# A square root on ScalarE and a reciprocal on VectorE in place of Ln and Exp, in all RMS norms of a three-block kernel

## The chip, the cores and the metric

The kernel runs on one core of a Trainium2 chip. The metric is the device time of one execution in microseconds (us), taken as the median of several runs; lower is better. The engines are named as in the profile: PE is TensorE, ACT is ScalarE, DVE is VectorE, POOL is GpSimd and SP is SyncE, which issues the DMAs here.

## The reference

Three different residual blocks are applied one after the other to x, 512 tokens by 1024 channels, in float32: one with a gated linear recurrence and a convolution, one with three mixers, one with two delta-rule recurrences. Before each mixer or feed-forward part, and at the end of each block, the rows of x are normalised; inside the third block the 64-wide heads of some tensors are normalised too (to unit length, or to unit mean square). All of these have one core:

```python
def _rmsnorm(x, g):
    xf = x.astype(jnp.float32)
    y = xf * lax.rsqrt(jnp.mean(xf * xf, axis=-1, keepdims=True) + EPS)
    return (y * g.astype(jnp.float32)).astype(x.dtype)

def _modulate(x, g, shift, scale):
    return _rmsnorm(x, g) * (1 + scale) + shift
```

## The kernel before

Channels lie on the 128 partitions and the 512 tokens on the free axis, so that x is `K.xT` with 8 slices of 128x512, and its normalised, modulated copy is `K.hT`. The program is a row of phases. Each phase is a `Block` with one instruction list for each engine, and the order within each list is that of the code. The next block's work starts when every engine has ended its list of this one, so a phase costs what its slowest engine costs. Semaphores order the engines within a phase.

Two helpers are concerned. `norm_phase` normalises whole rows. It is called nine times: at the start of the first block (there with two jobs, x of width 512 and the context of width 256), before its second mixer and at its end; at the start of the second block, before its MLP and at its end; and the same three places of the third block. At the start of the third block POOL builds masks for the recurrences in the same phase (`on_pool`). A phase runs so: ACT loads an activation table (L394) and squares the 8 slices (L400); PE sums over the partitions with a matrix of ones (L420); ACT takes Ln of the mean (L404) and Exp of -0.5 times that (L406), which is 1/sqrt; DVE multiplies the 8 slices by the gain and by that factor (L435); ACT adds the shift (L411), except in the final norms.

`head_norm_phase` does the same for heads, with one 128x512 slice as a job: `nk3` has 4 jobs, `lnx` 4 (with a subtraction of the mean first, L2154), `l2` 8 and `on` 4. For job n ACT squares (L2144), PE sums (L2127), ACT does Ln (L2135) and Exp in place (L2137) into one of two buffers `rs`, DVE multiplies (L2157). ACT squares job n+1 before it takes the root of job n. After `nk3` and after `l2` comes `delta_phase`, whose ACT list begins with Exp activations (L2365, L2360); after the first `norm_phase` comes `hgrn_phase`, whose ACT list begins with an Exp (L617). None of these three has a table load of its own in the code.

`preload_act_table_set` asks for a table load by name. Where the code asks for none, the compiler places the loads.

Of the kernel before, what the change touches and what calls it, by code (L numbers as in the profile page):

```python
# [9 lines left out]
ACT = mybir.ActivationFunctionType  # L10
AX = mybir.AxisListType
P = 128
DM = 1024
# [4 lines left out]
LOG_EXP_SET = "natural_log_exp_and_others"  # L18
# [41 lines left out]
def clear_old(sp, old):  # L60

    for s in old:
        sp.sem_clear(s)
# [305 lines left out]
def norm_phase(K, jobs, on_pool=None):  # L369


    nc = K.nc
    with ExitStack() as st:
        sq = K.sb(st, "norm_sq", [P, 2, T])
        gain = K.sb(st, "norm_gain", [P, len(jobs), KD])
        root = K.sb(st, "norm_root", [P, len(jobs), T])
        rstd = K.sb(st, "norm_rstd", [P, len(jobs), T])
        ps = K.psum_banks(st, "norm")
        sems, old = K.phase()
        squared, summed, rooted, inverted, gained, scaled, added, chain = sems[:8]  # L380
        wide = K.sb(st, "norm_masks", [P, 9, P]) if on_pool else None
        with nc.Block() as block:
            @block.sync
            def _(sp):
                clear_old(sp, old)

            if on_pool:
                @block.gpsimd
                def _(pool):
                    on_pool(K, pool, wide, *sems[8:11])  # L390

            @block.scalar
            def _(act):
                act.preload_act_table_set(LOG_EXP_SET)  # L394
                n = 0
                for j, (x, dst, w, *_) in enumerate(jobs):
                    for k in range(KD):
                        if n >= 2:
                            act.wait_ge(summed, n - 1)
                        act.activation(sq[:, n % 2, 0:w], x[:, k, 0:w], ACT.Square).then_inc(squared, 1)  # L400
                        n += 1
                for j, (x, dst, w, *_) in enumerate(jobs):
                    act.wait_ge(summed, KD * (j + 1))
                    act.activation(root[:, j, 0:w], ps[j][:, 0:w], ACT.Ln, scale=1.0 / DM, bias=K.epsc[:, 0:1]).then_inc(rooted, 1)  # L404
                    act.wait_ge(rooted, j + 1)
                    act.activation(rstd[:, j, 0:w], root[:, j, 0:w], ACT.Exp, scale=-0.5).then_inc(inverted, 1)  # L406
                for j, (x, dst, w, g, shift, scale, v) in enumerate(jobs):
                    if shift is not None:
                        for k in range(KD):
                            act.wait_ge(scaled, KD * j + k + 1)  # L410
                            act.activation(dst[:, k, 0:w], dst[:, k, 0:w], ACT.Identity,  # L411
                                           bias=K.mod[:, shift + k, v:v + 1]).then_inc(added, 1)

            @block.tensor
            def _(pe):
                n = 0
                for j, (x, dst, w, *_) in enumerate(jobs):
                    for k in range(KD):
                        pe.wait_ge(squared, n + 1)
                        pe.matmul(ps[j][:, 0:w], K.ones[:, :], sq[:, n % 2, 0:w], start=(k == 0), stop=(k == KD - 1)).then_inc(summed, 1)  # L420
                        n += 1

            @block.vector
            def _(dve):
                for j, (x, dst, w, g, shift, scale, v) in enumerate(jobs):
                    if shift is None:
                        dve.tensor_copy(gain[:, j, :], K.vec[:, g:g + KD]).then_inc(gained, 1)
                    else:
                        dve.scalar_tensor_tensor(gain[:, j, :], K.mod[:, scale:scale + KD, v], 1.0, K.vec[:, g:g + KD],
                                                 ALU.add, ALU.mult).then_inc(gained, 1)  # L430
                dve.wait_ge(gained, len(jobs))
                for j, (x, dst, w, g, shift, scale, v) in enumerate(jobs):
                    dve.wait_ge(inverted, j + 1)
                    for k in range(KD):
                        dve.scalar_tensor_tensor(dst[:, k, 0:w], x[:, k, 0:w], gain[:, j, k:k + 1], rstd[:, j, 0:w],  # L435
                                                 ALU.mult, ALU.mult).then_inc(scaled, 1)
# [1664 lines left out]
def head_norm_phase(K, tag, jobs, eps, mean_of, center=False):  # L2101


    nc = K.nc
    with ExitStack() as st:
        sq = K.sb(st, tag + "_sq", [P, 2, T])
        rs = K.sb(st, tag + "_rs", [P, 2, T])
        ps = K.psum_banks(st, tag)
        sems, old = K.phase()
        mean, cen, sqd, summed, root, inv, done = sems[:7]  # L2110
        with nc.Block() as block:
            @block.sync
            def _(sp):
                clear_old(sp, old)

            @block.tensor
            def _(pe):
                if center:
                    for n, (x, _) in enumerate(jobs):
                        if n >= 2:  # L2120
                            pe.wait_ge(cen, n - 1)
                        pe.matmul(ps[n % 2][:, :], K.two[:, :], x, start=True, stop=True).then_inc(mean, 1)
                for n in range(len(jobs)):
                    pe.wait_ge(sqd, n + 1)
                    if n >= 2:
                        pe.wait_ge(root, n - 1)
                    pe.matmul(ps[2 + n % 2][:, :], K.two[:, :], sq[:, n % 2, :], start=True, stop=True).then_inc(summed, 1)  # L2127

            @block.scalar
            def _(act):  # L2130
                def root_of(n):
                    act.wait_ge(summed, n + 1)
                    if n >= 2:
                        act.wait_ge(done, n - 1)
                    act.activation(rs[:, n % 2, :], ps[2 + n % 2][:, :], ACT.Ln, scale=1.0 / mean_of, bias=eps[:, 0:1]).then_inc(root, 1)  # L2135
                    act.wait_ge(root, n + 1)
                    act.activation(rs[:, n % 2, :], rs[:, n % 2, :], ACT.Exp, scale=-0.5).then_inc(inv, 1)  # L2137
                act.preload_act_table_set(LOG_EXP_SET)
                for n, (x, _) in enumerate(jobs):
                    if center:  # L2140
                        act.wait_ge(cen, n + 1)
                    if n >= 2:
                        act.wait_ge(summed, n - 1)
                    act.activation(sq[:, n % 2, :], x, ACT.Square).then_inc(sqd, 1)  # L2144
                    if n >= 1:
                        root_of(n - 1)
                root_of(len(jobs) - 1)

            @block.vector
            def _(dve):  # L2150
                if center:
                    for n, (x, _) in enumerate(jobs):
                        dve.wait_ge(mean, n + 1)
                        dve.scalar_tensor_tensor(x, ps[n % 2][:, :], -1.0 / C, x, ALU.mult, ALU.add).then_inc(cen, 1)  # L2154
                for n, (x, gain) in enumerate(jobs):
                    dve.wait_ge(inv, n + 1)
                    dve.scalar_tensor_tensor(x, x, gain, rs[:, n % 2, :], ALU.mult, ALU.mult).then_inc(done, 1)  # L2157

# [528 lines left out]
```

## Time and profile before

| | |
|---|---|
| median of 3 runs | 4726.74 us (4717.89 to 4729.1) |
| the profiled execution | 4729.1 us, span 4727.4 us |
| PE busy | 4004.8 us, 85% of the span |
| DVE busy | 1669.1 us, 35% |
| ACT busy | 1308.1 us, 28% |
| POOL busy | 603.2 us, 13% |
| granted PE clock, mean | 0.905 of full |

The span is what the profiler's records cover; the time lies 1.7 us above it. The share of an engine is a mean over phases with very different limits.

### The profile page before, as it was taken

Reading aid. Unit: us, or ns where it says so; the run is one execution under the profiler, and the core shown is the slowest. Engines: PE = TensorE matmul, PEld = TensorE weight load, DVE = VectorE, ACT = ScalarE, POOL = GpSimd, SP = SyncE. Lnnn points to the kernel's source line nnn. Section 1 sums busy time; section 2 is a strip of 40 time slices with the busy share of each in tenths; the row PEclk is TensorE's granted clock in tenths of the full one; section 3 lists DMA queues with packets and bytes.
Section 4 is the critical chain, followed back from the end, with each engine's and each line's share of the span. In section 5 each row is a group of like instructions: output and inputs, shape, how many; then the busy total and the mean of one; then the engine's idle time right before and its main releaser. Section 6 shows DMA issues by size and latency. Waiting matters only on the chain. (4 is left out here: it accounts for less than half of the span.)

```text
span 4727.4 us, 61028 instructions
## 1 busy us (share of the span) xinstructions
PE 4004.8 (85%) x23891; PEld 2693.9 (57%) x23891; DVE 1669.1 (35%) x3008; ACT 1308.1 (28%) x2192; POOL 603.2 (13%) x326
## 2 busy tenths in 40 slices
PE   6789999999689997778889977988678667877987
PEld 2356666666464443344465555866438447665765
DVE  1024444444516994123213322111227455032222
ACT  0133333333421122222113333222331231324322
POOL 0000000000020000010000022433410110333432
PEclk7799999999899998889869988988889789988998
DMA  8921111111024220112021112322110100222322
GB/s 319 352 62 41 40 44 40 41 44 44 18 58 120 72 71 18 50 36 58 16 55 45 28 53 76 98 76 71 40 29 3 46 10 21 71 71 80 92 72 67
DMA packets 484430, 312.98 MB, mean 66 GB/s; under 512 B 28236, under 2 KB 441477, under 8 KB 484262
## 3 DMA queue, kind: packets, MB, share of 16 engines
q1 hardware_dynamic: 484262, 310.67, 22.3%
q8 instruction: 113, 1.85, 0.2%
q14 instruction: 55, 0.45, 0.0%
HBM read 308.54 MB, written 2.10 MB: 66 GB/s over the span
## 5 line engine op out<-in xcount | busy, mean ns | idle before, releaser
L541 PE MATMUL hg_bank<-hT,hg_w 128*128 128x512 f32 x1024 | 447.3, 592 | 0.0
L998 PE MATMUL cv_bank<-hT,cv_w 128*128 128x512 f32 x768 | 334.0, 596 | 14.1 <-DMA cv_w<-in_conv_w_in_dram 14.1
L541 PEld LDWEIGHTS hg_bank<-hT,hg_w 128*128 128x128 f32 x1024 | 193.3, 190 | 223.6 <-issue 221.9
L1072 DVE SCALAR_TENSOR_TENSOR conv_u<-cv_pad,vec,conv_u 128x512 f32<-128x512 f32 x480 | 318.7, 743 | 0.0
L998 PEld LDWEIGHTS cv_bank<-hT,cv_w 128*128 128x128 f32 x768 | 146.8, 191 | 199.7 <-issue 184.8
L850 PE MATMUL m_bank<-m_rh,m_wh 128*128 128x512 f32 x512 | 205.0, 400 | 63.9 <-POOL m_wl L834 63.9
L851 PE MATMUL m_bank<-m_rl,m_wh 128*128 128x512 f32 x512 | 203.6, 398 | 0.0
L852 PE MATMUL m_bank<-m_rh,m_wl 128*128 128x512 f32 x512 | 203.4, 397 | 0.0
L834 POOL TENSOR_TENSOR m_wl<-m_w,m_wh 128x1024 fp32r<-128x1024 f32 x64 | 152.5, 2386 | 286.3 <-ACT m_wh L866 286.3
L1675 PE MATMUL at_bank<-hT,at_w 128*128 128x512 f32 x384 | 177.1, 605 | 0.0
L834 POOL TENSOR_TENSOR ho_wl<-ho_w,ho_wh 128x2048 fp32r<-128x2048 f32 x8 | 36.6, 4578 | 1079.3 <-ACT ho_wh L866 1079.3
L850 PE MATMUL ff_bank<-ff_rh,ff_wh 128*128 128x512 f32 x352 | 139.1, 395 | 32.8 <-POOL ff_wl L834 32.8
L755 DVE COPY hg_probe<-hg_bank 128x1 f32<-128x1 f32 x32 | 5.1, 158 | 447.0 <-PE hg_bank L556 447.0
L850 PEld LDWEIGHTS m_bank<-m_rh,m_wh 128*128 128x128 f32 x512 | 99.2, 194 | 87.4 <-issue 66.4
L852 PE MATMUL ff_bank<-ff_rh,ff_wl 128*128 128x512 f32 x352 | 137.9, 392 | 0.0
L851 PE MATMUL ff_bank<-ff_rl,ff_wh 128*128 128x512 f32 x352 | 137.9, 392 | 0.0
L537 PE MATMUL hg_bank<-hg_w,hT 128*128 128x128 f32 x1024 | 119.3, 278 | 16.5 <-DMA hg_w<-in_hgrn_w_in_dram 16.5
L537 PEld LDWEIGHTS hg_bank<-hg_w,hT 128*128 128x128 f32 x1024 | 119.1, 195 | 24.1 <-DMA hg_w<-in_hgrn_w_in_dram 16.9
L834 POOL TENSOR_TENSOR ff_wl<-ff_w,ff_wh 128x1024 fp32r<-128x1024 f32 x44 | 104.0, 2384 | 181.9 <-ACT ff_wh L866 181.9
L420 PE MATMUL norm_bank<-norm_sq,ones 128*128 128x512 f32 (+1 forms) x160 | 90.0, 721 | 40.8 <-ACT norm_sq L400 40.5
L1380 PE MATMUL ml_bank<-hT,ml_w 128*128 128x512 f32 x256 | 118.9, 616 | 3.6 <-ACT ml_o L1442 3.0
L314 PE MATMUL ada_bank<-ada_w,ada_cond 128*32 128x512 f32 x480 | 90.5, 893 | 32.2 <-DMA ada_w<-in_w_ada_dram 26.2
(668 smaller groups left out, 8001.3 us busy)
## 6 DMA issues: line engine op xcount, KB each, us to landing
ada_w<-in_w_ada_dram SPq DMA_DIRECT2D x24, 2048.0 KB, 19.6
hg_w<-in_hgrn_w_in_dram SPq DMA_DIRECT2D x80, 512.0 KB, 3.7
m_w<-in_w_mlp_dram SPq DMA_DIRECT2D x64, 512.0 KB, 4.1
ada_w<-in_ada_w_dram SPq DMA_DIRECT2D x12, 2048.0 KB, 19.8
cv_w<-in_conv_w_in_dram SPq DMA_DIRECT2D x48, 512.0 KB, 3.9
ff_w<-in_w_ffn_in_dram SPq DMA_DIRECT2D x44, 512.0 KB, 4.9
at_w<-in_w_in_dram SPq DMA_DIRECT2D x24, 512.0 KB, 3.9
fo_w<-in_w_ffn_out_dram SPq DMA_DIRECT2D x16, 704.0 KB, 4.7
```

Source lines behind the costliest of these rows:

```text
L314: ins = pe.matmul(ps[s][g:g + 32, :], cond[:, k, :], w[s][:, k, :], start=(k < COLS), stop=(k >= KD - COLS))
L420: pe.matmul(ps[j][:, 0:w], K.ones[:, :], sq[:, n % 2, 0:w], start=(k == 0), stop=(k == KD - 1)).then_inc(summed, 1)
L537: ins = pe.matmul(bank[:, t * P:(t + 1) * P], src[:, k, t * P:(t + 1) * P], W[m][:, k, :], start=(k == 0), stop=(k == KD - 1))
L541: ins = pe.matmul(bank[:, 0:w], W[m][:, k, :], src[:, k, 0:w], start=(k == 0), stop=(k == KD - 1))
L834: ins = pool.tensor_tensor(WL[s % 2][g][:, :, :], W[s % raws][g][:, :, :], WH[s % 2][g][:, :, :].bitcast(F32), ALU.subtract)
L850: pe.matmul(ps[p * 4 + g][:, :], WH[p][g][:, k, :], rh[:, k, :], start=(k == 0), stop=False)
L851: pe.matmul(ps[p * 4 + g][:, :], WH[p][g][:, k, :], rl[:, k, :], start=False, stop=False)
L852: ins = pe.matmul(ps[p * 4 + g][:, :], WL[p][g][:, k, :], rh[:, k, :], start=False, stop=(k == kt - 1))
L998: ins = pe.matmul(ps[n % RING][:, :], W[n % SLOTS][:, k * P:(k + 1) * P], K.hT[:, k, :], start=(k == 0), stop=(k == KD - 1))
L1072: ins = dve.scalar_tensor_tensor(o, x, by, o, ALU.mult, ALU.add)
L1380: ins = pe.matmul(SIDE_BANK[n % 2][:, :], W[n % WS][:, k, :], K.hT[:, k, :], start=(k == 0), stop=(k == KD - 1))
L1675: ins = pe.matmul(SIDE_BANK[:, :], W[n % WS][:, k, :], K.hT[:, k, :], start=(k == 0), stop=(k == KD - 1))
```

## The change

In both helpers the explicit load of the table set with Ln and Exp goes, Ln and Exp become one Sqrt on ACT, and DVE takes the reciprocal of its result ahead of the multiplications, and waits for its own reciprocal.

```diff
@@ norm_phase
-                act.preload_act_table_set(LOG_EXP_SET)
...
                     act.wait_ge(summed, KD * (j + 1))
-                    act.activation(root[:, j, 0:w], ps[j][:, 0:w], ACT.Ln, scale=1.0 / DM, bias=K.epsc[:, 0:1]).then_inc(rooted, 1)
-                    act.wait_ge(rooted, j + 1)
-                    act.activation(rstd[:, j, 0:w], root[:, j, 0:w], ACT.Exp, scale=-0.5).then_inc(inverted, 1)
+                    act.activation(root[:, j, 0:w], ps[j][:, 0:w], ACT.Sqrt, scale=1.0 / DM, bias=K.epsc[:, 0:1]).then_inc(rooted, 1)
...
                 for j, (x, dst, w, g, shift, scale, v) in enumerate(jobs):
+                    dve.wait_ge(rooted, j + 1)
+                    dve.reciprocal(rstd[:, j, 0:w], root[:, j, 0:w]).then_inc(inverted, 1)
                     dve.wait_ge(inverted, j + 1)
@@ head_norm_phase
-                    act.activation(rs[:, n % 2, :], ps[2 + n % 2][:, :], ACT.Ln, scale=1.0 / mean_of, bias=eps[:, 0:1]).then_inc(root, 1)
-                    act.wait_ge(root, n + 1)
-                    act.activation(rs[:, n % 2, :], rs[:, n % 2, :], ACT.Exp, scale=-0.5).then_inc(inv, 1)
-                act.preload_act_table_set(LOG_EXP_SET)
+                    act.activation(rs[:, n % 2, :], ps[2 + n % 2][:, :], ACT.Sqrt, scale=1.0 / mean_of, bias=eps[:, 0:1]).then_inc(root, 1)
...
                 for n, (x, gain) in enumerate(jobs):
+                    dve.wait_ge(root, n + 1)
+                    dve.reciprocal(rs[:, n % 2, :], rs[:, n % 2, :]).then_inc(inv, 1)
                     dve.wait_ge(inv, n + 1)
```

## Rows read from the trace of the kernel before

**Rows 1.** The page: busy time, share of the span, instructions.
```profile
PE 4004.8 (85%) x23891; PEld 2693.9 (57%) x23891; DVE 1669.1 (35%) x3008; ACT 1308.1 (28%) x2192; POOL 603.2 (13%) x326
```
**Rows 2.** Timeline, two `norm_phase` in turn: start, duration, instruction, [idle before <-releaser].
```profile
3333.48 1.28 ACT L394 ACT_TABLE_LOAD   x1 [11.03 <-PEq L813]
...
3344.58 0.69 ACT L404 ACTIVATE norm_root<-norm_bank,epsc 128x512 f32<-128x512 f32 x1 [1.22 <-PE norm_bank L420]
3345.30 0.63 ACT L406 ACTIVATE norm_rstd<-norm_root 128x512 f32<-128x512 f32 x1
3346.05 5.39 DVE L435 SCALAR_TENSOR_TENSOR xT<-xT,norm_gain,norm_rstd 128x512 f32<-128x512 f32 x8 [12.36 <-ACT norm_rstd L406]
...
3351.72 1.28 ACT L394 ACT_TABLE_LOAD   x1 [5.79 <-PEq L382]
...
3366.32 5.70 ACT L411 ACTIVATE hT<-hT,mod 128x512 f32<-128x512 f32 x8 [0.89 <-DVE hT L435]
...
3376.77 0.38 POOL L252 TENSOR_SCALAR neg_up_strict<-up_strict 128x64 f32<-128x64 f32 x1
```
**Rows 3.** Single lines of the kernel: reciprocals, ns min/median/max, first and last start.
```profile
L1517 DVE RECIPROCAL merge_gate<-merge_gate x4: 3353/3353/3353, 2204.6 to 2288.6; 128x512 f32<-128x512 f32 x4
L692 DVE RECIPROCAL hg_lb<-hg_tmp x1: 353/353/353, 260.0 to 260.0; 128x32 f32<-128x32 f32 x1
```
**Rows 4.** Timeline of DVE around a reciprocal in `mlstm_phase`.
```profile
2273.93 3.35 DVE L1517 RECIPROCAL merge_gate<-merge_gate 128x512 f32<-128x512 f32 x1
2277.31 0.69 DVE L1519 TENSOR_TENSOR merge_gate<-ml_bank,merge_gate 128x512 f32<-128x512 f32 x1
```
**Rows 5.** Timeline of `nk3`, 4 jobs: first instructions and last multiplication.
```profile
3532.15 1.28 ACT L2138 ACT_TABLE_LOAD   x1 [12.31 <-PEq L2169]
3533.44 1.15 ACT L2144 ACTIVATE nk_sq<-rw_kk 128x512 f32<-128x512 f32 x2
...
3536.24 0.69 ACT L2135 ACTIVATE nk_rs<-nk_bank,epsc 128x512 f32<-128x512 f32 x1 [1.65 <-PE nk_bank L2127]
3536.96 0.63 ACT L2137 ACTIVATE nk_rs<-nk_rs 128x512 f32<-128x512 f32 x1
...
3542.46 0.69 DVE L2157 SCALAR_TENSOR_TENSOR rw_kk<-rw_kk,nk_rs 128x512 f32<-128x512 f32 x1 [0.63 <-ACT nk_rs L2137]
```
**Rows 6.** Timeline of `l2`, 8 jobs: first Ln, last multiplication.
```profile
3835.25 0.69 ACT L2135 ACTIVATE l_rs<-l_bank,epsc 128x512 f32<-128x512 f32 x1 [1.65 <-PE l_bank L2127]
...
3848.49 0.69 DVE L2157 SCALAR_TENSOR_TENSOR gdn_qkv<-gdn_qkv,l_rs 128x512 f32<-128x512 f32 x1 [0.64 <-ACT l_rs L2137]
```
**Rows 7.** Timeline of `lnx`, 4 jobs.
```profile
3689.03 1.28 ACT L2138 ACT_TABLE_LOAD   x1 [0.49 <-PEq L2232]
3690.92 0.63 ACT L2144 ACTIVATE lnx_sq<-rwkv_y 128x512 f32<-128x512 f32 x1 [0.61 <-DVE rwkv_y L2154]
...
3693.82 0.69 ACT L2135 ACTIVATE lnx_rs<-lnx_bank,eps 128x512 f32<-128x512 f32 x1 [1.41 <-PE lnx_bank L2127]
...
3700.93 0.75 DVE L2157 SCALAR_TENSOR_TENSOR rwkv_y<-rwkv_y,vec,lnx_rs 128x512 f32<-128x512 f32 x1 [1.46 <-ACT lnx_rs L2137]
```
**Rows 8.** Timeline of ACT: loads that the compiler placed, in `token_phase` and a product phase.
```profile
2055.70 0.72 ACT L1193 ACTIVATE tk_sq<-gm_v,tk_sums 128x512 f32<-128x512 f32 x1
...
2056.53 1.28 ACT L1195 ACT_TABLE_LOAD   x1
...
3745.41 1.28 ACT L1936 ACT_TABLE_LOAD   x1 [3.59 <-DVE gdn_qkv L1944]
```
**Rows 9.** Timeline of `delta_phase` after `nk3`: last Exp of slice 0, and DVE.
```profile
3548.68 0.61 ACT L2369 ACTIVATE rw_E<-rw_E 128x512 f32<-128x512 f32 x1
...
3550.28 0.69 DVE L2277 SCALAR_TENSOR_TENSOR rw_EA<-rw_EA,rw_kk 128x512 f32<-128x512 f32 x1
3550.88 0.69 DVE L2278 TENSOR_TENSOR rw_lw<-rw_lw,rw_p 128x512 f32<-128x512 f32 x1
```
**Rows 10.** Windows: busy us of PE, PEld, DVE, ACT, POOL; PEclk; DMA.
```profile
3378.00:3390.00 12.00, 2.77 (x7) 2.23 (x8) 4.92 (x9) 5.86 (x10) 4.66 (x2) 0.50 0.46 126
```

## The prediction

> **What bounds the kernel now.** The page comes first: PE is busy for 85% of the span and DVE for 35% [rows 1]. That average would say that work given to DVE is free. The timeline of a norm phase, read next, says otherwise. In it the reader should follow one path: Ln starts at 3344.58 and ends at 3345.27, Exp ends at 3345.93, DVE's first multiplication starts at 3346.05 after 12.36 us of idling for just that result, its eight end at 3351.44, and at 3351.72 the next phase begins [rows 2]. Nothing else runs meanwhile. So between phases there is no overlap, and what bounds a norm phase is a chain through ACT, PE, ACT and DVE. Whatever the change adds to this chain is added to the time. The same holds in `nk3`: the last Exp's user starts at 3542.46 and the phase ends with it [rows 5].
>
> **The price of a reciprocal.** The kernel already has this instruction in this shape: 128x512 in float32 took 3353 ns four times out of four, and 128x32 took 353 ns [rows 3]. Per element that is (3353 - 353) / 480 = 6.25 ns, so 128x256 comes to about 353 + 224 x 6.25 = 1753 ns (an estimate from these two rows). The user of a reciprocal starts 0.03 us after its end, the semaphore included: 2273.93 + 3.353 = 2277.28, and 2277.31 [rows 4]. Sqrt is taken at the cost of Ln, 0.69 us: same operands, same shape; the trace has no wide Sqrt, but all wide activations on these rows lie between 0.61 and 0.69 us, so the doubt is below 0.1 us per phase.
>
> **`norm_phase`.** Before, from the end of Ln to the first multiplication: 3346.05 - 3345.27 = 0.78 us, of which 0.12 is the step from ACT to DVE [rows 2]. After: 0.12 + 3.353 + 0.03 = 3.50 us. Net +2.72 us for a phase. Of the nine:
> - Seven plain ones: 7 x 2.72 = 19.0 us.
> - The first has a second job, of width 256. DVE works through job 0's eight multiplications before it comes to the second reciprocal, so that lies on the path whole: 2.72 + 1.75 + 0.03 = 4.5 us.
> - The one at the start of the third block costs nothing: ACT's last addition ends at 3372.02, while POOL, building masks in the same phase, ends at 3377.15 [rows 2]. The cover is 5.1 us. If it were gone, the price would be 2.7 us.
>
> Together 23.5 us.
>
> **`head_norm_phase`.** Here every job needs a reciprocal. Before, a job took ACT some 1.7 us (13.24 us from the first Ln to the eighth multiplication [rows 6], less 1.4 for the lead of one job: Ln, Exp and the step to DVE, over 7) and DVE waited for it; after, DVE needs 3.353 + 0.03 + 0.61 = 3.99 us a job where a multiplication takes 0.69 (independent DVE instructions of that length follow each other at 0.60 us [rows 9]; 0.61 is taken) and 4.05 where it takes 0.75 (they follow at (5.39 - 0.75) / 7 = 0.66 [rows 2]; 0.67 is taken). ACT's shortened job, with Exp gone, fits easily under that, and two buffers are enough, since Sqrt of the next job needs 0.69 us while a 3.35 us reciprocal runs. DVE becomes the bound. The end is the end of the first Sqrt + 0.03 + jobs x 3.99 (4.05) + 0.08, the last term because the last multiplication is not overlapped.
> - `nk3`: 3536.93 + 0.03 + 15.97 + 0.08 = 3553.0, before 3543.15 [rows 5]: +9.9 us.
> - `l2`: 3835.94 + 0.03 + 31.94 + 0.08 = 3868.0, before 3849.18 [rows 6]: +18.8 us.
> - `on` has the pattern of `nk3`, with the same 6.22 us from first Ln to last multiplication, and multiplications of 0.75: 0.69 + 0.03 + 16.21 + 0.08 against 6.22 + 0.75 = +10.0 us.
> - `lnx`: like `on`, but its load moves from a hidden place to an open one (below): first Sqrt ends at 3693.82 + 1.28 + 0.69 = 3695.79, so the end is 3712.1, before 3701.68 [rows 7]: +10.4 us.
>
> Together 49.1 us.
>
> **The table loads.** Thirteen explicit loads go, each 1.28 us, and the load of the set with Sqrt is now the compiler's to place. The trace shows where it puts one: directly ahead of the first activation that the present set lacks, behind that activation's wait. In `token_phase` Squares run on the earlier set and the load stands between the last Square and the Sqrt; in a product phase the load starts only after a 3.59 us wait for the data of its Silu [rows 8]. So here it should stand between the wait for PE's sum and Sqrt, open on the path. At the start of `nk3` the removed load is open too, since the Squares follow it at once [rows 5]: -1.28 + 1.28 = 0, and so in most phases. Exceptions: in `lnx` the removed load was half hidden, and the first Square waited for DVE 0.61 us longer anyway [rows 7], so nothing is gained there and 1.28 us is paid (counted above). The second of two norm phases in a row reloads a set that is already there [rows 2]; its load now falls away. That holds for the first norm of the second and third blocks, and for the final norm of the second, behind an MLP whose ACT list needs only Copy and Relu. The third block's is covered by POOL. Gain: 2 x 1.28 = 2.6 us. On the other side three Exp activations lose the set they relied on: L617, a small preparation while the first weights load, nothing; L2365 in `delta_phase`, where the last Exp of slice 0 ends at 3549.29 and DVE turns to its user at 3550.28 without waiting [rows 9]: 3549.29 + 1.28 + 0.03 - 3550.28 = 0.3 us; L2360, where DVE's preparation is as long, 0 to 0.3 us, taken as 0. The bound for these three is 0 to 3.8 us.
>
> What a load costs beside its own length is one point to weigh. After the load in `nk3` the next activation starts 0.01 us after its end (3533.43, 3533.44 [rows 5]). The Trainium skill (ScalarE: Activation LUTs, section "What ACT_TABLE_LOAD costs") gives 1283 ns for the load, which agrees, and adds a drain, 2.66 us for each switch. By that the two saved and the one exposed load would count double, and the sum would be about 1 us smaller. The same page (section "Table sets: the hidden batching unit") speaks against this change: Ln and Exp share one set, and Exp with Sqrt needs two. This trace prices that as the exposed loads just counted.
>
> **The sum.** 23.5 + 49.1 - 2.6 + 0.3 = 70.3 us against the profiled execution's 4729.1 us: 4799.4. This execution is 0.05% above the median of 4726.7, so by the median it would be 4797. I take 4799 us, 1.5% slower.
>
> **The rivals.**
> - *Loads at better places.* If the load runs while ACT waits for PE, each phase whose removed load was open gains 1.28 us: nine such waits, 11.5 us, 4788 us. For it: such an idle wait exists, 1.22 to 1.65 us long [rows 2, 5]. Against: rows 8, where the load came after the wait.
> - *More loads.* If Square is missing in a set that is now active (the sets left behind by Exp, Silu or Sigmoid), the phase gets a load ahead of the Squares as well as one ahead of Sqrt: up to 13 x 1.28 = 16.6 us, 4816 us. Against: Squares in `token_phase` ran on a set left by another function [rows 8].
> - *PE colder.* PE idles some 10 to 20 us longer in the head norms. If work behind them starts at a lower clock, DVE waits for PE in `delta_phase`: an estimate of 0 to 6 us, 4805 us at most. Against: a product phase behind a norm starts at a granted clock of 0.50, the 1.2 GHz level, already now [rows 10], so there is nothing to lose there.
> - *Not slower.* If this reciprocal, on data that Sqrt just wrote, were as fast as DVE's multiplications, 0.69 us, a norm phase would pay 0.06 us for it, DVE's job in a head norm would be 1.33 to 1.39 us against 1.7 now, and with the loads the sum would be about -5 us: 4724, no measurable difference. It decides at 70.3 / 28.5 = 2.47 us less than 3.353, that is below 0.9 us (28.5 reciprocals of full width on the path: 8, a half, and 20). Against: four out of four at 3353 ns, and a narrow one on the same line through them [rows 3].
>
> **How the numbers follow.** The forecast has a chance of 0.74 (4793 to 4806), the better places 0.08, more loads 0.08, the colder PE 0.07, not slower 0.03. Runs of before spread from 4717.9 to 4729.1 us, and a measurement of this kernel tells about 0.3%, 14 us, from no change. The range goes down to the better places less 2 us, 4786, and up close to more loads, 4814. Slower by over 0.3%: 0.97; within: 0.02; faster: 0.01.
>
> **What the profile after would show.** Nine or ten reciprocals of `norm_rstd` and 20 of the `rs` buffers, 3.35 us each in width 512; 3.5 us from the end of Sqrt to the first multiplication; DVE nearly without idle time from the first reciprocal to the last multiplication of a head norm, and 28.5 x 3.35 = some 96 us more on DVE; ACT less by about 18 us; loads at L404 or L2135 behind the wait, no load in the norm phases at the start and the end of the second block and at the start of the third; the norm at the third block's start no longer than before. PE's busy time should not move. The prediction falls if a reciprocal takes clearly less than 3.35 us, if a phase's end turns out to be set by something other than DVE, or if loads appear in the loops of the phases between.

## The result

The changed kernel takes 4781.4 us (median of 4 runs, 4777.7 to 4785.9) against 4726.2 us before: a ratio of 1.012, 95% interval 1.0109 to 1.0133. It is 55 us slower where 73 were forecast by the median (4799 us). The direction is right, and the time lies just under the low end of the range, 4786. The profiled execution is 4788.3 us, 59.2 above the profiled one of before; that pair is what the following accounts for.

The page of the kernel after, busy time, share of the span and instructions, as in [rows 1]:
```profile
PE 4003.1 (84%) x23891; PEld 2695.7 (56%) x23891; DVE 1770.8 (37%) x3038; ACT 1289.8 (27%) x2162; POOL 603.5 (13%) x326
```
DVE has 30 instructions more and 101.7 us more work, ACT 18.3 us less. Single lines of the kernel after, ns min/median/max and first and last start:
```profile
L431 DVE RECIPROCAL norm_rstd<-norm_root x10: 1746/3352/3353, 249.7 to 4767.2; 128x512 f32<-128x512 f32 x9, 128x256 f32<-128x256 f32 x1
L2153 DVE RECIPROCAL l_rs<-l_rs x8: 3344/3346/3353, 3865.9 to 3893.8; 128x512 f32<-128x512 f32 x8
L403 ACT ACT_TABLE_LOAD  x6: 1283/1283/1283, 247.6 to 4765.1; - x6
L2134 ACT ACT_TABLE_LOAD  x4: 1283/1283/1283, 3541.5 to 4036.5; - x4
```
The reciprocals cost what [rows 3] say, and the loads are as many as the forecast had: six in nine norm phases, one in each of the four head norms. What is new is when they run. Timeline of the norm phase ahead of the second mixer, kernel before (it follows busy PE work):
```profile
1394.08 1.28 ACT L394 ACT_TABLE_LOAD   x1 [21.05 <-PEq L813]
1395.37 1.15 ACT L400 ACTIVATE norm_sq<-xT 128x512 f32<-128x512 f32 x2
...
1405.18 0.69 ACT L404 ACTIVATE norm_root<-norm_bank,epsc 128x512 f32<-128x512 f32 x1 [1.22 <-PE norm_bank L420]
```
The same phase after:
```profile
1399.13 1.15 ACT L399 ACTIVATE norm_sq<-xT 128x512 f32<-128x512 f32 x2 [21.07 <-PEq L812]
...
1405.53 0.63 ACT L399 ACTIVATE norm_sq<-xT 128x512 f32<-128x512 f32 x1 [0.23 <-PE norm_bank L417]
1406.17 1.28 ACT L403 ACT_TABLE_LOAD   x1
1407.47 0.69 ACT L403 ACTIVATE norm_root<-norm_bank,epsc 128x512 f32<-128x512 f32 x1
1408.27 3.35 DVE L431 RECIPROCAL norm_rstd<-norm_root 128x512 f32<-128x512 f32 x1 [8.94 <-ACT norm_root L403]
1411.65 5.39 DVE L434 SCALAR_TENSOR_TENSOR hT<-xT,norm_gain,norm_rstd 128x512 f32<-128x512 f32 x8
```
Two things are to be seen. The load starts at 1406.17, straight behind the last Square, with no idle time before it, and it covers the 1.22 us in which ACT waited for PE before. Secondly, from the phase's start to the root it took 11.10 us before and takes 8.34 now: 2.76 less, more than one load of 1.28. The rest is PE's clock. Windows over these two stretches (columns as in [rows 10]), before and then after:
```profile
1394.10:1405.20 11.10, 9.09 (x16) 3.12 (x16) 0.17 (x1) 6.21 (x10) 0.00 (x0) 0.85 0.00 1
```
```profile
1399.10:1407.50 8.40, 7.52 (x16) 2.46 (x16) 0.17 (x1) 6.24 (x10) 0.00 (x0) 1.00 0.00 1
```
One microsecond out of the middle of the first of them:
```profile
1398.00:1399.00 1.00, 1.00 (x3) 0.50 (x2) 0.00 (x0) 0.05 (x1) 0.00 (x0) 0.50 0.00 0
```
PE's sums in both kernels, with its idle time ahead of them:
```profile
1396.05 9.09 PE L420 MATMUL norm_bank<-norm_sq,ones 128*128 128x512 f32 x16 [3.28 <-ACT norm_sq L400]
```
```profile
1399.82 7.52 PE L417 MATMUL norm_bank<-norm_sq,ones 128*128 128x512 f32 x16 [2.01 <-ACT norm_sq L399]
```
Before, the sixteen records of the sums take 9.09 us at a mean granted clock of 0.85 for the stretch, part of them at 0.50, the 1.2 GHz level; after, 7.52 us at 1.00, the 2.4 GHz level throughout. PE stands idle 2.01 us instead of 3.28 between the product before and its first sum. Not every phase gains this. Six norm phases follow busy PE work and have a start like this one, 11.1 us to the root in nearly all of them before. In the first profile of the changed kernel four of the six take 8.3 us to the root, in a second one three; the others take 9.8 to 10.0. From the root to the first multiplication the forecast holds: 1411.65 - 1408.16 = 3.49 us (3.50 forecast).

`nk3` after, the counterpart of [rows 5], and the start of the `delta_phase` behind it:
```profile
3540.38 1.15 ACT L2140 ACTIVATE nk_sq<-rw_kk 128x512 f32<-128x512 f32 x2 [12.45 <-PEq L2167]
...
3541.54 1.28 ACT L2134 ACT_TABLE_LOAD   x1
...
3542.84 0.69 ACT L2134 ACTIVATE nk_rs<-nk_bank,epsc 128x512 f32<-128x512 f32 x1
...
3543.56 3.35 DVE L2153 RECIPROCAL nk_rs<-nk_rs 128x512 f32<-128x512 f32 x1 [3.48 <-ACT nk_rs L2134]
...
3546.95 0.69 DVE L2155 SCALAR_TENSOR_TENSOR rw_kk<-rw_kk,nk_rs 128x512 f32<-128x512 f32 x1
3547.56 3.34 DVE L2153 RECIPROCAL nk_rs<-nk_rs 128x512 f32<-128x512 f32 x1
...
3558.91 0.69 DVE L2155 SCALAR_TENSOR_TENSOR rw_kk<-rw_kk,nk_rs 128x512 f32<-128x512 f32 x1
3559.89 1.28 ACT L2363 ACT_TABLE_LOAD   x1 [7.47 <-PEq L2110]
...
3563.45 0.63 ACT L2363 ACTIVATE rw_EA<-rw_EA 128x512 f32<-128x512 f32 x1 [2.28 <-DVE rw_E L2264]
```
DVE runs without a gap from the first reciprocal on, 3.99 us a job, as forecast. The first root comes 2.46 us after the start, against 4.09 in [rows 5]. The load for Exp, forecast behind its wait at 0.3 us, runs at once when the phase begins and ACT then idles 2.28 us more: it costs nothing.

The whole, from the two timelines. Each of the 13 norm and head-norm phases is cut at its start (its first instruction), its first root, its first multiplication and its end (the end of its last instruction). The last row also holds what lies ahead of the first norm phase, where nothing was changed; that stretch alone is 1.5 us longer here.

| | difference after - before | forecast |
|---|---|---|
| start to first root | -20.9 us | -2.6 for two loads, +1.3 for `lnx` |
| first root to first multiplication | +35.0 us | together with the next row 71.3, |
| first multiplication to end | +37.4 us | with nothing for the phase under POOL |
| everything ahead of, between and behind the phases | +7.7 us | +0.3 |
| sum | +59.2 us | +70.3 |

### The profile page after: what moved, and what is told of

It reads as the page before. It is cut to its first block and busy times, and to the rows that moved or that the text cites. A ratio compares the mean times of both kernels' runs of the same rounds, so it can differ in the third digit from the quotient of the medians.

```text
span 4786.6 us, 61028 instructions
## 1 busy us (share of the span) xinstructions
PE 4003.1 (84%) x23891; PEld 2695.7 (56%) x23891; DVE 1770.8 (37%) x3038; ACT 1289.8 (27%) x2162; POOL 603.5 (13%) x326
## 5 line engine op out<-in xcount | busy, mean ns | idle before, releaser
L540 PE MATMUL hg_bank<-ctxT,hg_w 128*128 128x256 f32 x512 | 115.7, 379 | 0.0
## 6 DMA issues: line engine op xcount, KB each, us to landing
ada_w<-in_w_ada_dram SPq DMA_DIRECT2D x24, 2048.0 KB, 19.6
```

The lines of the kernel that those rows point to most:

```text
L540: ins = pe.matmul(bank[:, 0:w], W[m][:, k, :], src[:, k, 0:w], start=(k == 0), stop=(k == KD - 1))
```

## Experiments

Each is compared with runs of the kernel before on its own chip (4728.95 us in the first four, 4728.41 in the next three). Theory A says that the shortfall comes from where the load stands: hidden in ACT's wait, and with PE reached sooner and so still at its higher clock. Its rivals are B (placement is worth nothing) and C (only the wait, not the clock).

**The load moved, Ln and Exp kept.** Only the explicit load of the kernel before moves.
```diff
-                act.preload_act_table_set(LOG_EXP_SET)      # norm_phase: ahead of the Squares
+                act.preload_act_table_set(LOG_EXP_SET)      # behind them, ahead of wait_ge(summed, ...)
...
+                    if n == 1:                              # head_norm_phase: ahead of the first root
+                        act.preload_act_table_set(LOG_EXP_SET)
```


> The kernel before, with Ln and Exp kept, and only the explicit table load moved: in norm_phase from ahead of the Squares to behind them, in head_norm_phase to just ahead of the first Ln. No reciprocal. Theory A (the shortfall against the forecast comes from where the load stands: it now runs while ACT waits for PE, and PE starts 1.28 us sooner after the phase before and so keeps its clock): about 20 us faster than before, 4702 to 4710 us, and from phase start to first Ln 8.3 us in the norm phases that follow busy PE work, against 11.1. Theory B (the placement is worth nothing, the shortfall comes from other phases or from variation between executions): 4720 to 4730 us. Theory C (only the idle wait is used, the clock stays as it was): 10 to 13 us faster, 4714 to 4717.

4716.9 us, ratio 0.9975 (0.9965 to 0.9985): faster by 12, beating both kernels. Timeline of the same norm phase, and windows over it:
```profile
1395.80 1.15 ACT L399 ACTIVATE norm_sq<-xT 128x512 f32<-128x512 f32 x2 [21.07 <-PEq L813]
...
1402.85 1.28 ACT L401 ACT_TABLE_LOAD   x1
1404.14 0.69 ACT L404 ACTIVATE norm_root<-norm_bank,epsc 128x512 f32<-128x512 f32 x1
```
```profile
1395.80:1404.20 8.40, 7.52 (x16) 2.46 (x16) 0.17 (x1) 6.27 (x10) 0.00 (x0) 1.00 0.00 1
```
8.34 us from start to root, with the clock at 1.00: A's mechanism with no Sqrt and no reciprocal in sight. The 13 phases gained 23 us up to their first root. But the time fell by only 12, so A's number (4702 to 4710) missed; C's number fits while its claim about the clock does not. Of the other 11 us, 3.6 are lost inside the phases, between the first multiplication and the end: the phase under POOL, where POOL ends last, is only 0.5 us shorter for a root 2.5 us sooner, and `nk3` and `on` end only 0.7 us sooner for a root 1.6 us sooner. The rest is lost outside them, and is taken up below.

**The load put back at the start of the changed kernel.**
```diff
+                act.preload_act_table_set(SQRT_SET)         # "sqrt_and_others", first in ACT's list, both helpers
```


> The changed kernel with one thing put back: an explicit load (of the set with Sqrt) at the start of both helpers, where before had its own. Theory A: the 22 us that the phases gained between their start and the first root go again, 4799 to 4806 us, close to the forecast for the change. Theory B: no change, 4778 to 4786 us. Theory C: 4793 us.

4804.1 us, ratio 1.0157 (1.0143 to 1.0171). The same phase:
```profile
1398.66 1.28 ACT L395 ACT_TABLE_LOAD   x1 [21.05 <-PEq L814]
...
1409.76 0.69 ACT L405 ACTIVATE norm_root<-norm_bank,epsc 128x512 f32<-128x512 f32 x1 [1.22 <-PE norm_bank L419]
```
```profile
1398.70:1409.80 11.10, 9.09 (x16) 3.12 (x16) 0.17 (x1) 6.21 (x10) 0.00 (x0) 0.85 0.00 1
```
11.10 us and 0.85 again, and the time is 75 us above before where the changed kernel is 55 above. That lies in A's range and outside those of B and C. The kernel has a load in all 13 phases, three more than the changed one; its price is near the one that the forecast gave to the change.

**The load written out behind the wait**, where the forecast had put it.
```diff
                     act.wait_ge(summed, KD * (j + 1))
+                    if j == 0:
+                        act.preload_act_table_set(SQRT_SET)  # and likewise for job 0 in head_norm_phase
```


> The changed kernel with the load of the set with Sqrt written out, behind the wait for PE's sum, where the forecast put it; in the three norm phases that needed no load there is one now. It parts the two halves of Theory A: PE starts early as in the changed kernel, but the load is not hidden. If hiding the load is worth 1.2 us in each of ten phases with a load, and the three new ones cost 1.3 us in two places (the third lies under POOL): 4791 to 4797 us. If all of the gain were the clock: 4780 to 4785 us.

4795.0 us, ratio 1.0144 (1.0129 to 1.016), in the range named for "hiding counts". Timeline of the same phase:
```profile
1396.24 1.15 ACT L400 ACTIVATE norm_sq<-xT 128x512 f32<-128x512 f32 x2 [21.06 <-PEq L815]
...
1404.47 1.28 ACT L405 ACT_TABLE_LOAD   x1 [1.21 <-PE norm_bank L420]
1405.77 0.69 ACT L406 ACTIVATE norm_root<-norm_bank,epsc 128x512 f32<-128x512 f32 x1
```
Here the load does wait 1.21 us, and start to root is 9.53 us: the clock's 1.57 are gained, the wait's 1.20 are not. The kernel has three loads that the changed kernel does not have. Two of them are open, at the start and at the end of the second block, and its starts there are 1.0 and 1.3 us longer than in the first profile of the changed kernel.

**PE kept busy during the old load.** Kernel before, with filler matmuls ahead of `norm_phase`'s own.
```diff
+                for k in range(4):
+                    pe.matmul(ps[7][:, 0:256], K.ones[:, :], jobs[0][0][:, k, 0:256], start=True, stop=True)
```


> The kernel before, load at its old place, and four matmuls of 128x256 on data at hand ahead of norm_phase's own, into a bank that nobody reads, so that PE is not idle during the load (head_norm_phase is left as it was). It parts the clock from the wait. Theory A: PE's sums run at a granted clock near 1.0 in the phases behind busy PE work, some 1.5 us less in four to six phases, 5 to 9 us faster than before: 4717 to 4722 us. Theory C: 4726 us or a little more. If the filler itself delays the first sum: up to 1 us more a phase, 4735.

4725.7 us, ratio 0.9992 (0.9983 to 1.0001): not told from no change. By its time A missed (4717 to 4722) and C's number fits. In the phase, though, the effect is there:
```profile
1394.67 1.28 ACT L394 ACT_TABLE_LOAD   x1 [21.05 <-PEq L815]
...
1404.21 0.69 ACT L404 ACTIVATE norm_root<-norm_bank,epsc 128x512 f32<-128x512 f32 x1 [1.22 <-PE norm_bank L422]
```
```profile
1394.70:1404.30 9.60, 9.46 (x24) 3.88 (x24) 0.17 (x1) 6.28 (x10) 0.00 (x0) 1.00 0.00 1
```
The load is in its old place, the wait of 1.22 is still there, and yet start to root is 9.54 us. That is the clock alone. All six phases that follow busy PE work take 9.53 us. All phases together gained 11.8 us by this profile, and the interval of its time allows at most 8 of them.

**The reciprocals alone.**
```diff
-                    dve.reciprocal(rstd[:, j, 0:w], root[:, j, 0:w]).then_inc(inverted, 1)   # and rs; DVE reads root itself
-  ... ACT.Sqrt, scale=1.0 / DM, ...
+  ... ACT.Sqrt, scale=0.0, ...
```


> The changed kernel without its reciprocals: DVE multiplies by the output of Sqrt itself, and Sqrt is fed scale 0.0, so that the factor is a constant and values stay bounded. What is left out is the reciprocal and with it the normalisation. It prices the reciprocals alone. If each costs what its timeline shows (8 of 3.38 us and one of 1.78 us in the norm phases, 20 jobs that fall from 3.99 to about 1.2 us in the head norms): 85 us less than the changed kernel, 4694 to 4700 us. If part of the reciprocal's time is given back elsewhere, for instance because PE rests longer and is granted more clock later: less than 75 us, above 4706.

4700.5 us, ratio 0.9936 (0.9922 to 0.995): 81 us under the changed kernel by the medians, 87 by the two ratios (0.0184 x 4726), for 85 expected; the time lies at the upper end of the range named (4700). First and last multiplication of `nk3`:
```profile
3522.88 0.69 DVE L2151 SCALAR_TENSOR_TENSOR rw_kk<-rw_kk,nk_rs 128x512 f32<-128x512 f32 x1 [3.81 <-ACT nk_rs L2132]
...
3527.01 0.69 DVE L2151 SCALAR_TENSOR_TENSOR rw_kk<-rw_kk,nk_rs 128x512 f32<-128x512 f32 x1 [0.63 <-ACT nk_rs L2132]
```
4.13 us for three jobs, where the changed kernel needs 11.96. So a root on ACT with nothing behind it is faster than Ln and Exp; the reciprocal on DVE is what makes the change slow. (This kernel's output is not normalised: it gives a price and is no alternative.)

**Half the change.** Each helper changed alone.

> norm_phase as changed, head_norm_phase as before. By the forecast's terms (every reciprocal on the path, 7 x 2.72 + 4.5, less 2.6 for loads): 21 us slower than before. By Theory A (in the trace of the changed kernel the nine phases lose about 23 us to reciprocals that are not covered by POOL, and gain 16 us between their start and the first root): 6 to 10 us slower, and within what the profile's other stretches vary.

> head_norm_phase as changed, norm_phase as before. By the forecast's terms: 49 us slower than before. By Theory A (48 us for the reciprocals by the trace, less 5.6 us between start and first root): 42 us slower, plus what the delta phases lose when PE comes to them colder, 0 to 6 us.

`norm_phase` alone: 4740.8 us, ratio 1.0025 (1.0016 to 1.0034), 12 us. `head_norm_phase` alone: 4768.4 us, ratio 1.0091 (1.0075 to 1.0106), 40 us. The forecast had 21 and 49, Theory A 6 to 10 and 42; the first lies 2 us above A's range. Together the halves make 52 of the 55 us, so they add. Three quarters of the loss are the 20 jobs of the head norms.

**Repeated profiles**, to find out what the stretches between the phases are.

> The kernel before once more, for a second profile: by how much the stretches between the norm phases vary from one execution to the next. If the 9.6 us that these stretches took longer in the profile of the changed kernel are variation, this one differs from the first profile by some us too; if they are an effect of the change, it agrees with the first within 2 us.

> The kernel of late_load once more, for a second profile. Its phases gained 23 us between their start and the first root, its time only 12. If the rest (9 us in the stretches between the phases) is given back there because of the change, this profile shows the same 9 us, against a new profile of before; if it is variation, the stretches sum to within 4 us of those of before.

> As the run before this one: a third profile of the same kernel, same expectations.

> The kernel before for a third profile, to which the two are compared: the sum of its stretches between the phases within 4 us of the first two profiles of before.

> The changed kernel for a second profile. Between start and first root the phases take the same as in the first profile within 3 us; if the 8 us more in the stretches between are an effect of the change they are here again, if variation they are not.

Their times: before 4726.8 and 4725.5, the moved load 4714.7 and 4723.1, the changed kernel 4787.4 us. Sums from the timelines, us; the last column holds everything outside the 13 phases:

| kernel, profiles | start to first root | outside the phases |
|---|---|---|
| before, 3 | 124.6, 124.6, 126.0 | 4491.9, 4490.3, 4487.7 |
| load moved, 3 | 101.4, 101.4, 99.9 | 4500.0, 4497.2, 4507.0 |
| changed, 2 | 103.7, 102.9 | 4499.6, 4498.7 |

Both columns hang on the kernel more than on the execution, which moves the second by up to 10 us (one stretch of before took 924.5 us in the first profile and 920.0 and 919.5 in the others). The expectation for the third profile of before, within 4 us of the other two, missed by 0.2. Against the mean of before, 4490.0, part of the gain up to the root is given back each time: 10, 7 and 17 us with the load moved, 10 and 9 in the changed kernel. The stretch ahead of the first norm phase moves by itself between 231.3 and 235.6 us. Without it, before takes 4259.7, 4256.0 and 4254.8, the kernel with the moved load 4265.9, 4265.9 and 4271.4, and the changed kernel 4265.8 and 4265.1. But `norm_phase` alone (4258.3), `head_norm_phase` alone (4253.1) and the changed kernel with its load behind the wait (4258.1) give nothing back, while the changed kernel without reciprocals (4265.6) and the one with its load at the start (4264.4) do, each in one profile. One place is the `delta_phase` behind `l2`: 136.9 to 137.1 us in all three profiles of before, 139.4 in all three with the load moved. Windows of 30 us over the same part of it, before and then with the load moved:
```profile
3864.20:3894.20 30.00, 20.41 (x506) 19.59 (x504) 16.18 (x27) 8.70 (x17) 0.00 (x0) 0.82 0.01 2
```
```profile
3853.20:3883.20 30.00, 21.73 (x440) 20.76 (x438) 15.49 (x26) 8.10 (x16) 0.00 (x0) 0.67 0.01 2
```
PE is busy for longer, gets 66 records less done, and is granted 0.67 instead of 0.82. The code of this phase is the same. Cut into pieces of 5 us, the three in which PE is busiest (4.3 to 5.0 us) are granted 0.70 to 0.75 before and 0.50 with the load moved. But it is no law of this edit: the kernel with only `norm_phase` changed took 134.7 us there, less than before. Why the clock is higher in one kernel than in another at the same code is open; no run moved one such phase by itself.

## Why the prediction was wrong

- **The reciprocal's price: right.** 3353 ns, 1746 for width 256 (1753 estimated), 3.49 us from root to multiplication, 3.99 us a job. The two stretches behind the root sum to 72.4 us; the forecast's terms for them sum to 71.3. The 72.4 hold 1.7 of the phase under POOL, which as a whole grew by 0.1 us only: POOL still ended last there (3384.21 against 3380.22 for ACT), as forecast.
- **DVE as the bound of the head norms: right.** `nk3` lost 8.2 us, `on` 8.4 and `l2` 17.5, against 9.9, 10.0 and 18.8; each difference is the 1.3 to 1.6 us gained ahead of the first root.
- **The step that failed: "So here it should stand between the wait for PE's sum and Sqrt, open on the path."** The load ran ahead of the wait in all ten phases that have one, 0.02 us behind the Square before it. The forecast read its rule off one row, the load at L1936 after 3.59 us of waiting [rows 8], in a phase with a loop. The rival "loads at better places" had this mechanism, at a chance of 0.08 and 11.5 us. The kernel with the load behind the wait prices it: 66.6 us against 55.3 above before, 11.3 us, of which some 2.3 are its two extra open loads. That leaves about 9 us for the placing.
- **The step that was missing: the clock inside the norm phase.** The forecast looked for the clock only behind the phase, at rows 10, and only for a loss. It took the removal of a load at the start as worth 1.28 us. It is worth 1.28 plus, in three or four of the six phases that follow busy PE work, 1.57 us of PE time at a higher clock, as the filler shows by itself. Together with the step above, the starts gained 20.9 us where the forecast had 1.3. The four states of one phase are 11.10 us (load at the start), 9.53 (clock gained, load open), 9.90 (load hidden, clock not gained, as in the changed kernel's norm phase at 4312.7) and 8.34 us (both). The Trainium skill (TensorE: Matmul & The Clock Gate, Part 1) says that the clock follows how busy PE has been recently; the windows above agree, with 0.85 against 1.00.
- **`lnx`'s exposed load: wrong** by the same step. Its first root came 4.76 us after the start in the second profile of the changed kernel, where it was 4.79 before; in the first it took 6.45, but a kernel that has the load at the start also took 6.30 once (the third profile of before).
- **The second norm of a pair: right that the load fell away, wrong that it gains 1.28 us.** At the start of the second block start to root fell from 11.29 to 10.53 us, by 0.76: PE's sums took 9.81 us there instead of 9.27. A longer rest of PE through the reciprocal (10.68 us ahead of the sums instead of 9.13) does not explain it: with the load moved and no reciprocal the rest is 7.96 us and the sums take 9.78. Why they are slower when they start sooner is open. The final norm of the second block gained 1.29 us in one profile of the changed kernel and 2.86 in the other.
- **The loads ahead of Exp: a miss of 0.3 us.** They run when the phase starts.
- **More loads: no.** Ten loads and three ahead of Exp stand for the thirteen of before, none of them ahead of a Square.
- **Colder PE behind the head norms: there, but small.** In the first 15 us behind `nk3` and `l2` PE is granted 0.50, where it had 0.54 and 0.57 before; the two `delta_phase` took 146.4 and 137.5 us against 145.9 and 137.0, and 147.7 and 137.8 in the second profile of the changed kernel. Most of the 7.7 us outside the phases, against 0.3 forecast, lie elsewhere. 1.5 are ahead of the first norm phase, and the largest piece, 3.4 us, is behind `lnx`, where the first 30 us run at 0.50 in both kernels and only the products after them get 0.85 instead of 0.91. Neither half of the change shows that piece by itself, and its cause is open. So two errors partly cancel: the starts gave 19.6 us more than forecast, what lies outside the phases took 7.4 more, and the stretches behind the root 1.1 more. That the miss of 11.1 us is so near the 11.5 of the rival on loads is luck.
- **Not slower: refuted** by the reciprocal's duration, and its point of decision (2.5 us less for each) by the 81 to 87 us that they cost in all.

## What to carry to other kernels

Price an instruction on the chain, not by its engine's share of the span: DVE was at 35%, and 30 reciprocals added 1.7% on it. A table load cost most here at the very start of a phase, where it held up every engine behind it and in three or four of six phases cost PE its clock; put behind the work that feeds PE, and ahead of the wait for PE's answer, it cost less than 0.1 us, and that move alone made the kernel 0.25% faster. A saving inside one phase has to be looked for again in the total: here about half of it was lost again, a part inside the same phases and more of it outside them, at least partly as PE clock.

## What the runs showed of the hardware

In ten phases a load placed by the compiler ran ahead of the wait of the activation that needs it (1406.17, no idle time before it), while an explicit load written behind the wait waits itself (1.21 us). In the loop at L1936 the compiler's load did wait [rows 8]; why it stands differently there is not shown. A load took 1.28 us in all: it starts 0.02 us behind a Square, and the root follows 0.02 us behind its end (1406.17 + 1.28, 1407.47). So the drain that the prediction weighed does not show. A shift of 1.28 us in when PE starts after a phase boundary changed the granted clock of the stretch to the root from 0.85 to 1.00. With the load moved, five of the six starts concerned came out the same to 0.01 us in three profiles (8.34 us in four, 9.90 in one), and the sixth took 9.90, 9.90 and 8.34; in the changed kernel three of the six differed by 1.6 us from one profile to the next.
